# Mixer to FFN on Trainium2: the last output group by tiles, its sum of squares by column positions, the first residual tiles singly, ones matmuls on TensorE meanwhile, and mixer B's value products a step later

## What is computed

```python
h = rms_norm(x, g_pre_mix)                         # (264, 2048)
qa, ka, va, qb, kb, vb = split(h @ w_in)           # 4352 columns
o_a = sliding_window_attention(qa, ka, va, sinks)  # mixer A
o_b = dilated_attention(qb, kb, vb)                # mixer B, with 320 cached keys per request and head
o = concat(rms_norm(o_a, g_out_a), rms_norm(o_b, g_out_b))
x = x + rms_norm(o @ w_out, g_post_mix)
h = rms_norm(x, g_pre_ffn)
u, up = h @ w_gate, h @ w_up                       # 5632 columns each
x = x + rms_norm((gelu(causal_conv3(u)) * up) @ w_down, g_post_ffn)
```

## Time and profile before

| | |
|---|---|
| median of three runs | 1193.95 us (1193.79 to 1194.48) |
| the profiled execution, own time | 1196.02 us |
| its span, first to last instruction | 1194.2 us |
| TensorE matmul busy | 1168.1 us, 98% of the span |
| TensorE weight load busy | 1135.4 us, 95% |
| VectorE, ScalarE, GpSimd busy | 698.4, 554.4, 105.8 us |
| the chain of work that ended last | TensorE 93%, VectorE 3%, DMA 2%, ScalarE 1% |

### The profile page before, as it was taken

One profiled execution on the slowest core, in us unless ns is written; L12 is line 12 of the kernel. 1 busy time (PEld: TensorE's weight loads), 2 busy tenths in 40 slices (PEclk: granted clock), 3 DMA queues, 4 the chain that ended last, 5 costly groups with the idle time before them and its releaser, 6 DMA issues.

```text
span 1194.2 us, 25575 instructions
## 1 busy us (share of the span) xinstructions
PE 1168.1 (98%) x9947; PEld 1135.4 (95%) x9947; DVE 698.4 (58%) x1050; ACT 554.4 (46%) x859; POOL 105.8 (9%) x163
## 2 busy tenths in 40 slices
PE   9999999999999799999999999999999999999995
PEld 8999889988899799999999999999999999999995
DVE  5877565674375865655656565656565444454445
ACT  7455555565455654444444443444444433343331
POOL 0100111110002010011001000100110000020001
PEclk9999999999999899999999999999999999999998
DMA  8746677676555345555465555555555655555551
GB/s 309 208 142 226 235 252 235 213 228 234 168 172 180 107 144 193 180 178 183 162 201 168 191 157 196 168 184 170 182 181 182 205 182 176 178 184 183 177 158 72
DMA packets 59473, 222.21 MB, mean 186 GB/s; under 512 B 7064, under 2 KB 7264, under 8 KB 57312
## 3 DMA queue, kind: packets, MB, share of 16 engines
q1 hardware_dynamic: 55152, 196.58, 51.2%
q0 software_dynamic: 4272, 24.94, 6.2%
HBM read 216.45 MB, written 5.00 MB: 185 GB/s over the span
## 4 chain that ended last, share of the span: by engine, by line
PE 93%; DVE 3%; DMA 2%; ACT 1%; issue 1%; SPq 0%; POOL 0%; DVEq 0%; ACTq 0%
PE ps L1130 29%; PE ps L1131 29%; PE ps L1132 28%; PE ps L1301 1%; DMA Vk<-in_vb 1%; PE ps L1219 1%; DVE wl L681 1%; PE ps L1282 1%; DMA xT<-in_x 1%; PE ps L1210 1%; PE ps L1208 1%; PE ps L1237 0%; PE ps L1155 0%; DVE yT L977 0%; DVE ps L976 0%
## 5 line engine op out<-in xcount | busy, mean ns | idle before, releaser
L1130 PE MATMUL ps<-hh,wh 128*128 128x264 f32 x2080 | 600.1, 289 | 8.2 <-DVE hl L886 5.8
L1132 PE MATMUL ps<-hh,wl 128*128 128x264 f32 x2080 | 593.0, 285 | 0.0
L1131 PE MATMUL ps<-hl,wh 128*128 128x264 f32 x1952 | 557.7, 286 | 0.0
L681 DVE TENSOR_TENSOR wl<-raw,wh 128x1024 fp32r<-128x1024 f32 x363 | 438.4, 1225 | 192.2 <-ACT wh L424 191.7
L424 ACT CAST wh<-raw 128x1024 fp32r<-128x1024 f32 x363 | 374.6, 1046 | 275.4 <-PE ps L1132 272.0
L1130 PEld LDWEIGHTS ps<-hh,wh 128*128 128x128 f32 x2080 | 394.0, 189 | 20.5 <-issue 17.5
L1132 PEld LDWEIGHTS ps<-hh,wl 128*128 128x128 f32 x2080 | 392.8, 189 | 0.0
L1131 PEld LDWEIGHTS ps<-hl,wh 128*128 128x128 f32 x1952 | 368.7, 189 | 0.1
L1131 PE MATMUL ps<-gl,wh 128*128 (+1 forms) x704 | 200.4, 285 | 0.0
L1130 PE MATMUL ps<-gh,wh 128*128 (+1 forms) x704 | 200.1, 284 | 0.0
L1132 PE MATMUL ps<-gh,wl 128*128 (+1 forms) x704 | 199.6, 283 | 0.0
(11 more groups left out here) (229 smaller groups left out, 832.5 us busy)
## 6 DMA issues: line engine op xcount, KB each, us to landing
raw<-in_w_gate SPq DMA_DIRECT2D x88, 512.0 KB, 3.7
raw<-in_w_up SPq DMA_DIRECT2D x88, 512.0 KB, 4.6
raw<-in_w_down SPq DMA_DIRECT2D x88, 512.0 KB, 3.5
raw<-in_w_in SPq DMA_DIRECT2D x67, 512.0 KB, 4.8
raw<-in_w_out SPq DMA_DIRECT2D x32, 512.0 KB, 3.8
Kt<-in_kb POOLq DMA_DIRECT2D x8, 1284.0 KB, 6.2
Vk<-in_vb POOLq DMA_DIRECT2D x8, 1024.0 KB, 7.1
out_y<-yT SPq DMA_DIRECT2D x8, 264.0 KB, 2.1
```

The costliest lines, as they stand in the source:

```text
L681: V.tensor_tensor(wl[:, slot], raw[:, slot], wh[:, slot].bitcast(F32), ALU.subtract).then_inc(lo_ready, 1)
L1130: nc.tensor.matmul(out, a, x, start=start, stop=False)
L1131: nc.tensor.matmul(out, a, xl, start=False, stop=False)
L1132: return nc.tensor.matmul(out, b, x, start=False, stop=stop)
```

## The change

- In the plan, mixer B's `bV` and `bO` of every odd unit come one step later; `sq`, `N`, `NF` and `G` of mixer B follow by one step.
- The last output group runs tile by tile: all 24 matmuls of its first tile, then four 32-column ones matmuls (the squares so far, one per column position), then the 24 of its second tile. Each tile has its own VectorE add and ScalarE square. ScalarE copies the four-part sum to `rms`; one ones matmul adds it, one each the two last squares.
- TensorE then runs 16 matmuls of ones on ones (`hold_clock`).
- VectorE takes the first two residual tiles singly, the rest in pairs, and makes `hl` of a pair right behind its own add. Weight chunks 2 and 3 of the FFN are split before the residual, and the splits of later ones are placed anew (`ahead`).

```diff
-        for v, steps in enumerate(((-3, -2, 0, 4, 5), (1, 3, 6, 7, 8))):
+        for v, steps in enumerate(((-3, -2, 0, 4, 5), (1, 3, 6, 8, 9))):
             for kind, at in zip(("qsel", "bS", "bR", "bV", "bO"), steps):
                 add(e + at, kind, 2 * t + v)
-    for X, q, n in ((0, 0, 28), (0, 1, 42), (1, 0, 64), (1, 1, 76)):
+    for X, q, n in ((0, 0, 28), (0, 1, 42), (1, 0, 64), (1, 1, 77)):
         add(n, "sq", X, q)
         add(n + 1, "N", X, q)
     add(53, "NF", 0)
-    add(78, "NF", 1)
+    add(79, "NF", 1)
...
-        add(79 + j // 2, "G", 1, j, j + 2)
+        add(80 + j // 2, "G", 1, j, j + 2)
@@ ScalarE: the last group
+            split(chunk(B_OUTB, G_OUT // 2 - 1, 4, 5))
+            for m in range(2):
+                act.wait_ge(y_last, m + 1)
+                nc.scalar.activation(cv[:, m, 0:TOK], yT[:, MT - 2 + m], ACT.Square).then_inc(ysq_ready, 1)
+                if m == 0:
+                    act.wait_ge(ysum_ready, 1)
+                    nc.scalar.activation(rms[:], ps[:, B_M, 0:TOK], ACT.Copy, scale=1.0 / 32).then_inc(ypart_ready, 1)
+                    split(chunk(B_OUTB, G_OUT // 2 - 1, 4, 6))
+            act.wait_ge(ysq_ready, G_OUT + 1)
+            for j in (MT - 2, MT - 1):
+                ins = nc.scalar.activation(yT[:, j], yT[:, j], ACT.Copy, scale=par[:, C_GQM + j:C_GQM + j + 1])
...
             act.wait_ge(sum_ready, 1)
             nc.scalar.activation(rms[:], ps[:, B_M, 0:TOK], ACT.Sqrt, bias=eps[:], scale=1.0 / D_MODEL).then_inc(norm_a, 1)
+            split(chunk(B_GU, 0, 8, 3))
             for jj in range(MT // 2):
-                act.wait_ge(x1_ready, jj + 1)
                 for j in (2 * jj, 2 * jj + 1):
+                    act.wait_ge(x1_ready, j + 1 if jj == 0 else jj + 2)
                     nc.scalar.activation(hh[:, j], xT[:, j], ACT.Copy,
...
-                if jj:
+                if jj >= 2:
                     split(chunk(B_GU, 0, 8, jj + 2))
@@ VectorE: the last group
+            for j in range(2):
+                split(chunk(B_OUTB, G_OUT // 2 - 1, 4, 4 + j))
+            for m in range(2):
...
+                y1 = yT[:, MT - 2 + m]
+                V.tensor_tensor(y1, ps[:, 2 * ((G_IN + G_OUT + 1) % 2) + m, 0:TOK], y1, ALU.add).then_inc(y_last, 1)
+            split(chunk(B_GU, 0, 8, 2))
@@ VectorE: the residual
-            for jj in range(MT // 2):
-                y2, x2 = yT[:, 2 * jj:2 * jj + 2], xT[:, 2 * jj:2 * jj + 2]
-                line.step(V.tensor_tensor(y2, y2, wide(rB[:]), ALU.mult))
-                V.tensor_tensor(x2, x2, y2, ALU.add).then_inc(x1_ready, 1)
-                if jj:
-                    low(jj - 1)
-                if jj >= 2:
-                    split(chunk(B_GU, 0, 8, jj))
-            low(MT // 2 - 1)
+            residual(0, 1)
+            residual(1, 2)
+            low(0)
+            low(1)
+            ahead = {1: (3,), 3: (4,), 5: (5, 6), 7: (7,)}
+            for jj in range(1, MT // 2):
...
+                residual(2 * jj, 2 * jj + 2)
+                low(2 * jj)
+                low(2 * jj + 1)
+                for c in ahead.get(jj, ()):
+                    split(chunk(B_GU, 0, 8, c))
@@ TensorE
+            def hold_clock(n):
+                for k in range(n):
+                    nc.tensor.matmul(ps[:, 4, 0:P], ones[:], ones[:], start=True, stop=True)
...
-            sum_squares()
+            for m in range(2):
+                bank = 2 * ((G_IN + G_OUT + 1) % 2) + m
+                for c, (n, slot, _) in enumerate(ends):
+                    for k in range(4):
+                        ins = mm3(ps[:, bank, 0:TOK], (slot, 256 * k + P * m), hh[:, 4 * c + k], hh[:, OT + 4 * c + k],
+                                  c + k == 0, (c, k) == (1, 3))
...
+                if m == 0:
+                    ins.then_inc(y_tile, 1)
+                    pe.wait_ge(ysq_used, SUMS)
+                    pe.wait_ge(ysq_ready, G_OUT - 1)
+                    for j, x in enumerate((sqa[:, 0], sqa[:, 1], sq[:, 0], sq[:, 1])):
+                        ins = nc.tensor.matmul(ps[32 * j:32 * j + 32, B_M, 0:TOK], ones[:, 0:32], x, start=True, stop=True)
+                    ins.then_inc(ysum_ready, 1)
+            pe.wait_ge(ypart_ready, 1)
+            nc.tensor.matmul(ps[:, B_M, 0:TOK], ones[:], rms[:], start=True, stop=False)
+            for m in range(2):
+                pe.wait_ge(ysq_ready, G_OUT + m)
+                ins = nc.tensor.matmul(ps[:, B_M, 0:TOK], ones[:], cv[:, m, 0:TOK], start=False, stop=m == 1)
+            ins.then_inc(sum_ready, 1)
+            hold_clock(16)
```

More of the change, by code:

```diff
@@ L48 @@
 CHUNKS = N_IN + N_OUTA + N_OUTB + N_GU + N_DOWN
-SUMS = MT // 2
+SUMS = MT // 2 - 1
 OUT_V = 6
@@ L339, in build @@
         yg_ready, sqx_ready = sem("yg_ready"), sem("sqx_ready")
+        y_tile, y_last, ysum_ready, ypart_ready = (sem(n) for n in ("y_tile", "y_last", "ysum_ready", "ypart_ready"))
         stored, other_stored = sem("stored"), sem("other_stored")
@@ L587, in _, with out_b @@
             line.step(nc.scalar.activation(small[:, 100:101], eps[:], ACT.Sqrt))
-            with act.Fori(0, G_OUT // 2) as i:
+            def out_b(i, g):
+                for j in range(2):
+                    split(chunk(B_OUTB, i, 4, 2 * g + j + 3))
+                act.wait_ge(evac_done, i * 2 + (G_IN + G_OUT + g + 1))
+                act.wait_ge(ysq_used, i * 2 + (g + 1))
+                nc.scalar.activation(sq[:], yT[:, bass.ds(i * 4 + 2 * g, 2)], ACT.Square).then_inc(ysq_ready, 1)
+                act.wait_ge(ysq_ready, i * 2 + (g + 1))
+                for k in range(2):
+                    y1 = yT[:, bass.ds(i * 4 + (2 * g + k), 1)]
+                    ins = nc.scalar.activation(y1, y1, ACT.Copy, scale=par[:, bass.ds(i * 4 + (C_GQM + 2 * g + k), 1)])
+                    if k == 0:
+                        line.do(ins)
+                    else:
+                        ins.then_inc(yg_ready, 1)
@@ L589, in _ @@
+            with act.Fori(0, G_OUT // 2 - 1) as i:
                 line.loop(i, 2)
                 for g in range(2):
[L591 to L604, removed]
+                    out_b(i, g)
+            line.end(G_OUT // 2 - 1)
@@ new lines, in _ @@
+            out_b(G_OUT // 2 - 1, 0)
+            split(chunk(B_OUTB, G_OUT // 2 - 1, 4, 5))
[6 more added lines that the diff above has]
+                    split(chunk(B_OUTB, G_OUT // 2 - 1, 4, 6))
@@ L605, in _ @@
+            act.wait_ge(ysq_ready, G_OUT + 1)
+            for j in (MT - 2, MT - 1):
+                ins = nc.scalar.activation(yT[:, j], yT[:, j], ACT.Copy, scale=par[:, C_GQM + j:C_GQM + j + 1])
+                if j == MT - 2:
+                    line.do(ins)
+                else:
+                    ins.then_inc(yg_ready, 1)
             act.wait_ge(sum_ready, 1)
             nc.scalar.activation(rms[:], ps[:, B_M, 0:TOK], ACT.Sqrt, bias=eps[:], scale=1.0 / D_MODEL).then_inc(norm_a, 1)
+            split(chunk(B_GU, 0, 8, 3))
@@ L869, in _, with out_b @@
             dve.wait_ge(par_landed, 16)
-            with dve.Fori(0, G_OUT // 2) as i:
-                for g in range(2):
[L872 to L877, removed]
+            def out_b(i, g):
+                for j in range(2):
+                    split(chunk(B_OUTB, i, 4, 2 * g + j + 2))
+                dve.wait_ge(weights_used, i * 4 + (B_OUTB + 2 * g + 2))
+                b = 2 * ((G_IN + G_OUT + g) % 2)
+                y2 = yT[:, bass.ds(i * 4 + 2 * g, 2)]
+                V.tensor_tensor(y2, ps[:, b:b + 2, 0:TOK], y2, ALU.add).then_inc(evac_done, 1)
+            with dve.Fori(0, G_OUT // 2 - 1) as i:
+                for g in range(2):
+                    out_b(i, g)
+            out_b(G_OUT // 2 - 1, 0)
+            for j in range(2):
+                split(chunk(B_OUTB, G_OUT // 2 - 1, 4, 4 + j))
+            for m in range(2):
+                if m == 0:
+                    dve.wait_ge(y_tile, 1)
+                else:
+                    dve.wait_ge(weights_used, B_OUTB + N_OUTB)
+                y1 = yT[:, MT - 2 + m]
+                V.tensor_tensor(y1, ps[:, 2 * ((G_IN + G_OUT + 1) % 2) + m, 0:TOK], y1, ALU.add).then_inc(y_last, 1)
+            split(chunk(B_GU, 0, 8, 2))
             dve.wait_ge(norm_a, 1)
@@ L881, in _, with low, residual @@
             dve.wait_ge(rB_ready, 1)
[L883 to L889, removed]
-            for jj in range(MT // 2):
-                y2, x2 = yT[:, 2 * jj:2 * jj + 2], xT[:, 2 * jj:2 * jj + 2]
-                line.step(V.tensor_tensor(y2, y2, wide(rB[:]), ALU.mult))
-                V.tensor_tensor(x2, x2, y2, ALU.add).then_inc(x1_ready, 1)
-                if jj:
-                    low(jj - 1)
-                if jj >= 2:
-                    split(chunk(B_GU, 0, 8, jj))
-            low(MT // 2 - 1)
+            def low(j):
+                dve.wait_ge(h2h_ready, j + 1)
+                V.scalar_tensor_tensor(hl[:, j], xT[:, j], par[:, C_GPF + j:C_GPF + j + 1],
```

(36 more changed lines are left out.)

## The result

The changed kernel takes 1200.63 us in the median of ten runs (1198.82 to 1203.40), the kernel before 1193.80 in ten beside it (1193.29 to 1197.82). The ratio is 1.0057, 95% interval 1.0048 to 1.0065: 0.57% or 6.8 us slower. Of the kernel before, one execution beside experiments 5 to 8 took 1263.83 us at a granted clock of 0.846; ranges and ratios leave it out. The profiled execution took 1199.49 us, its span is 1197.7 us with a mean granted clock of 0.996. The ten executions differ in their clock: four took 1198.82 to 1199.49 us at a granted clock of 0.996, the other six 1200.53 to 1203.40 at 0.994 to 0.991.

What follows compares the result with a forecast made beforehand. TensorE, busy for 98% of the span, was taken as the bound. Terms -2.16 + 2.5 + 2.8 + 0.5 + 3.0 = +6.6 us, against the median 1193.95, gave 1200.6 us, range 1196.0 to 1203.5.

Steps and rivals of the forecast that it cites:

- The two stalls: Steps 53 and 65: TensorE waits for ScalarE's copy of bO behind S's exponentials, 2.8 us each; net +2.5 and +2.8.
- Rival D: The plan's stalls don't come, ScalarE copying bO ahead of the exponentials: 1192.3 us; chance 0.05, with C 0.02.
- The 2.16 us for the cached values: Mixer B's last unit: the value product, moved behind chunk 76, no longer waits for its load; gain 2.16 us.
- The clock: TensorE's clock falls in the two new mixer stalls: 1.5 us for each, 3.0 together.
- My bound of 2.4 for one stall: Clock loss measured between output and FFN, 2.4 us, taken as the bound from above for a mixer stall.
- rival B: Both stalls come, the clock stays full: 3.6 us, 1197.6; sign, a stall that leaves the clock full; chance 0.22.
- Rival E: Clock falls longer in both stalls, or at the junction too: 2.5 to 3.5 us each, 1203 to 1205; chance 0.07.
- The junction: Between output and FFN: TensorE starts 1.4 us earlier but gives it back waiting for VectorE; costs 0.5 us.
- VectorE's wait per pair: Residual between output and FFN: VectorE waits 0.66 us for ScalarE's hh in each of seven pairs.
- Rival C: VectorE's wait for hh is small, last quarter sum 4.2 us earlier: 1192.9 to 1195.9 us; chance 0.12.
- Ones on ones: Junction: 32 records take 3.6 us at full clock, 7.3 at half, hidden in TensorE's waits; price 0.
- The stretch in which there was something to win: Between output and FFN: some 11 us in which TensorE does 4; elsewhere only 2.16 us to win.

Runs made afterwards that it cites:

- experiment 5: The kernel before with only mixer B's last unit's value product, and sq, N, NF, G behind it, a step later: 1193.88 us, ratio 0.9999.
- experiment 6: The changed kernel with the plan of before and, from the second pair on, hl made a pair behind its add: 1195.35 us, ratio 1.0006.
- experiment 7: The changed kernel with the plan of before and five weight splits between a pair's add and its hl: 1191.85 us, ratio 0.9983.
- experiment 8: The changed kernel without the 16 ones-on-ones matmuls: 1200.94 us, ratio 1.0060.
- experiment 4: The changed kernel with 10 unused ones-on-ones matmuls on TensorE ahead of each of the two waits, NF(0) and N(1,0): 1198.92 us, ratio 1.0028.
- experiment 1: The kernel before with the change's plan alone, mixer B's odd value products a step later: 1202.23 us, ratio 1.0049.
- experiment 3: The changed kernel with bO ahead of S in steps 53 and 65 on all engines: 1194.18 us, ratio 0.9988.
- experiment 2: The changed kernel with the plan of before, so the rebuilt junction alone: 1195.27 us, ratio 1.0002.

## Why the prediction came out as it did

The predicted 1200.6 us and the measured 1200.63 agree better than their parts do. Point by point:

- **The two stalls** were right in place and cause and nearly in size: TensorE waits 2.5 and 2.6 us, where I had 2.8 each, and the wait of 0.3 us at 241 us vanished as said. Part of my 2.8, counted from one start of `NF` to the other, is TensorE's own work: the transposes now stand in it. Net I had 5.3 us for both; the traces give 4.9 (TensorE's lag, 0.5 at 36 us and 5.4 behind step 65). The executions in which the clock stayed give 5.3 (1199.1 against 1193.8), experiment 4 gives 5.1, with the difference between the sets in it. Experiment 1 shows that the stalls are the plan's, experiment 3 that they hang on the order `S`, `bO`. Rival D fell with it.
- **The 2.16 us for the cached values** was the step that failed: "Gain 2.16 us". The wait was in the profiled execution and at its full size not in the median execution (experiment 5, and the traces of 2 and 6). I had noted that this execution lay 2.1 us above the median, and I subtracted its wait from the median all the same. Against the median the term is small: 0.1 us the wrong way in experiment 5, whose interval leaves room for 1.2 us of gain. Where before had the higher median of 1194.99, later values may be worth 1 us (experiment 3 against 2, whose intervals overlap). There, the one execution of experiment 2 known to have had no wait is the fastest of its twelve (1193.65), 1.6 us under their median. What the later product does show is steadiness: experiment 5 spreads over 2.1 us, before beside it over 4.9 (1192.85 to 1197.78).
- **The clock** falls in the stalls, in part of the executions, as said. I took 3.0 us for both together; in the median it is 1.5 to 1.7, with 0 in the best and some 4.6 in the worst execution. My bound of 2.4 for one stall didn't hold: behind the second stall of experiment 1 it cost about 3.1. So rival B was right on the mechanism in four of ten executions (at 1199.1, not its 1197.6, as the gain for the values wasn't there), and the profile of the changed kernel shows the very sign that I had named for it. Rival E's longer fall came too, in experiment 1's second stall.
- **The junction** I priced at +0.5. Against the profiled execution of before it is +0.1 (42.8 to 42.9), from the last PSUM add to the last quarter sum 36.3 us where I had 36.7. The old junction itself took 42.9 in experiment 1 and 42.3 in experiment 5, and experiment 2's ratio, 1.0002, leaves 1 us either way. The mis-sized term is VectorE's wait per pair, 0.58 and not the 0.66 of the earlier trace rows: seven times 0.08 are 0.56. The cause is shown from both sides: filling five of the waits shortens the junction by 2.1 us (experiment 7), and the ones on ones change nothing while it stands (experiment 8). Rival C fell: its 4.2 us were never there, and even with the waits filled 1.3 us at tile 2 remain.
- **Ones on ones:** 32 records took 3.73 us (I said 3.6) and ended in TensorE's wait for `hl`; the price of 0 was right.
- **The stretch in which there was something to win** I put at some 11 us; its parts in my own rows (0.89 and 1.16, 5.75, and 5.3 for the chunk) are 13.1. No term of the sum goes by it.

With 0 for the values and the junction, 5.1 for the stalls and 1.7 for the clock the sum is 6.8 us. That it meets the measured 6.8 proves nothing, since 5.1 and 1.7 are its two parts as experiment 4's median divides it; the 4.9 from the traces is independent of it. Mine was 6.6: 2.2 too low for the values, 1.3 too high for the clock, 0.5 for the junction and 0.2 for the stalls. The closeness is luck in those four; that it would be slower, and where, was not.

## What to carry to other kernels

- Where several engines walk one list of stages, moving a stage puts it into every engine's list. Look not only at the engine that waited but at what stands ahead of the stage on the engine that frees its buffer: here four exponentials ahead of two small copies, in two of the four steps that were moved.
- Before subtracting a wait that a profile shows, set that execution's own time against the median. If the profiled execution is slower by just that wait, the median may have little or none of it; only a run settles how much.
- A turn from one engine to a second and back belongs behind other work of the first: 0.58 us, seven times, ate a junction's whole gain, and a reordering without any new instruction made it 2.3 us shorter (experiment 7 against 2). What is put in must be counted for the first use too (experiment 6).

## What the runs showed of the hardware

- Two silences of TensorE of 2.5 and 2.6 us cost nothing over their own length in some executions and up to 4.6 us more in others. In experiment 1's trace the granted clock is 0.50 from about their end on, for 3.4 and 6.8 us. With ones on ones in the silence the spread of the executions fell from 4.6 to 0.65 us.
- The same load of 256 KB behind 1 MB, issued at the same place, took 8.8 to 11.3 us to land in seven executions (8.8, 9.0, 9.0, 9.8, 9.9, 10.6, 11.3).
